# First attention of a two-block layer stack: outputs made transposed by pairs of heads, weights scaled before they are turned

## What is computed

```python
h = rms_norm(x, norm_gain);  proj = h @ w_in          # q, k, v, gates, z of both attentions
# NSA: 8 heads of 64 over 2 key groups, three branches
o_cmp = softmax(q kc^T, visible blocks) @ vc          # 32 compressed keys
o_sel = softmax(q ks^T, causal) @ vs                  # all 8 blocks are selected: plain causal
o_win = softmax(q kw^T, causal) @ vw                  # window 512: plain causal
nsa   = g0 * o_cmp + g1 * o_sel + g2 * o_win          # g: sigmoid gates per head and branch
# DSA: 8 heads, keys limited to the 128 best of an index score
dsa   = softmax(q_d k_d^T, causal and top 128) @ v_d
x     = x + concat(nsa * silu(z_n), dsa * silu(z_d)) @ w_out
```

## Time and profile before

| | us |
|---|---|
| median of 3 runs | 1799.81 (1799.48 to 1800.25) |
| the profiled execution | 1798.04 |
| its span in the trace | 1796.2 |
| first attention's loop on PE | 199.2 to 362.6 of the span |
| from there to the first matmul of the projection by w_out | 362.6 to 372.5 |
| projection by w_out | 372.5 to 424.5 |

### The profile page before, as it was taken

How to read it: one execution, slowest core, us unless ns; L and a number is a source line. 1 busy time by engine, 2 the same in 40 slices (tenths; PEclk the granted TensorE clock), 3 DMA queues, 4 the chain that set the end, 5 groups by cost and what they waited for, 6 DMA issues and landing times. The chain is left out here.

```text
span 1796.2 us, 23296 instructions
## 1 busy us (share of the span) xinstructions
PE 1734.0 (97%) x8345; PEld 1413.7 (79%) x8345; DVE 990.4 (55%) x1657; ACT 741.2 (41%) x1282; POOL 692.6 (39%) x301
## 2 busy tenths in 40 slices
PE   7999998988999999999999999999999999999997
PEld 7777787777888777788888888887776888888886
DVE  5999776475579687633333335789785631111112
ACT  6434555623375564322222223466464343222321
POOL 3424111236430234555545557440212544444442
PEclk9999999999999999999999999999999999999998
DMA  7234010053332224355555532332311222232211
GB/s 251 81 106 141 24 36 24 25 198 121 105 105 95 81 85 155 133 193 190 194 188 198 189 141 94 107 103 84 105 36 36 94 94 97 92 105 94 97 56 47
DMA packets 56633, 197.65 MB, mean 110 GB/s; under 512 B 6993, under 2 KB 8017, under 8 KB 56530
## 3 DMA queue, kind: packets, MB, share of 16 engines
q1 hardware_dynamic: 55666, 194.15, 31.8%
q10 hardware_dynamic: 864, 2.11, 0.3%
HBM read 194.14 MB, written 2.10 MB: 109 GB/s over the span
## 5 line engine op out<-in xcount | busy, mean ns | idle before, releaser
L513 POOL TENSOR_TENSOR WL<-RAW,WH 128x1024 fp32r<-128x1024 f32 x234 | 594.4, 2546 | 870.8 <-ACT WH L597 529.8
L1914 PE MATMUL bank<-HH,WH 128*128 128x512 f32 x1120 | 437.2, 390 | 9.5 <-POOLq L518 5.9
L1916 PE MATMUL bank<-HH,WL 128*128 128x512 f32 x1120 | 435.9, 389 | 0.0
L1915 PE MATMUL bank<-HL,WH 128*128 128x512 f32 x1120 | 435.8, 389 | 0.0
L597 ACT ACTIVATE WH<-RAW 128x1024 fp32r<-128x1024 f32 x259 | 270.6, 1052 | 244.2 <-PE bank L1916 220.0
L1914 PEld LDWEIGHTS bank<-HH,WH 128*128 128x128 f32 x1120 | 210.2, 188 | 55.1 <-issue 8.8
L1916 PEld LDWEIGHTS bank<-HH,WL 128*128 128x128 f32 x1120 | 210.2, 188 | 43.9
L1915 PEld LDWEIGHTS bank<-HL,WH 128*128 128x128 f32 x1120 | 210.3, 188 | 43.2
L1834 DVE TENSOR_TENSOR HF<-SILU,bank 128x512 f32<-128x512 f32 x43 | 29.6, 688 | 301.6 <-PE bank L1916 300.7
L1914 PE MATMUL bank<-HDH,WH 128*128 128x512 f32 x352 | 137.1, 389 | 0.0
L1916 PE MATMUL bank<-HDH,WL 128*128 128x512 f32 x352 | 136.9, 389 | 0.0
(11 more groups left out here) (371 smaller groups left out, 2934.5 us busy)
## 6 DMA issues: line engine op xcount, KB each, us to landing
RAW<-in_stream SPq DMA_DIRECT2D x363, 512.0 KB, 3.3
out_t<-YA SPq DMA_DIRECT2D x8, 256.0 KB, 2.2
X<-in_xt ACTq DMA_DIRECT2D x3, 512.0 KB, 10.9
RAW<-in_stream SPq DMA_DIRECT2D x2, 256.0 KB, 3.9
X<-in_xt ACTq DMA_DIRECT2D x2, 256.0 KB, 6.0
ACC<-in_pos SPq DMA_DIRECT2D x1, 256.0 KB
gains<-in_gains SPq DMA_DIRECT2D x1, 224.0 KB
CS<-in_cs SPq DMA_DIRECT2D x1, 128.0 KB
```

The source lines that it names most:

```text
L513: nc.gpsimd.tensor_tensor(lo(k)[:], raw(k)[:], hi(k)[:].bitcast(F32), ALU.subtract).then_inc(sem["passed"], mark("passed", *k))
L1914: nc.tensor.matmul(out, A[0], B[0], start=first, stop=False)
L1915: nc.tensor.matmul(out, A[0], B[1], start=False, stop=False)
L1916: return nc.tensor.matmul(out, A[1], B[0], start=False, stop=last)
```

## The change

- The units are ordered by head, then branch, then query tile, so that four units make one (head, branch) group. The weights of a unit are scaled by gate over sum while they still are in PR, before they are turned: by DVE for query tiles 0 and 1, by POOL for tiles 2 and 3. PR is a ring of eight, and the turn comes six turns behind the scores instead of three.
- The output of a whole group is four matmuls with V stationary (two columns of heads wide, the other head's columns zero in VZ) and the turned weights moving, 512, 384, 256 and 128 columns. Both heads of a pair and all branches accumulate in one bank, transposed, 128 by 512. The compressed branch is one matmul more per pair.
- Z is turned in the loop's turns 2 to 9, and DVE multiplies a pair's bank by it (`mix_pair_out`). MIX, its product on POOL and its turns are gone. High and low parts of a chunk are made as each pair ends, and the first matmuls of tiles 0 and 1 of the projection stand in the loop's last two turns.
- VZ has to be zero between the heads: POOL clears 128 x 3328 words before V is written.
- Compressed tiles start at turns 2, 6, 10, 14, the top-k rounds at turns 20 to 60. The 16 `ada` slots come in fours behind tiles 2 to 5 instead of in twos and threes behind tiles 0 to 5.

```diff
-        order += [ada.pop(0) for _ in range((2, 3, 3, 3, 3, 2, 0, 0)[n])]
+        order += [ada.pop(0) for _ in range((0, 0, 4, 4, 4, 4, 0, 0)[n])]
...
+UNITS1 = [(b, h % 4, h // 4, qt) for h in range(HEADS) for b in (0, 1) for qt in range(NT)]
+UNITS1 += [(2, h % 4, h // 4, qt) for h in range(HEADS) for qt in range(NT)]
+RING1, T_LAG1, O_LAG1 = 8, 6, 7
...
+def scaler(v):
+    return "p_norm" if v % NT < 2 else "p_pool"
+def mover(v):
+    return "read_dve" if v >= 20 and v % NT == 0 else "read_act"
+MIX_HI = {66: 0, 69: 1, 72: 2, 78: 3, 97: 4, 98: 5, 99: 6}
+MIX_LO_POOL = {66: 0, 69: 1, 72: 2, 77: 3}
+MIX_LO_DVE = {98: 4, 99: 5, 100: 6}
+O1_PASS = (76, 82, 90)
+O1_PARTS = {101: ((0, 0, 3),), 102: ((0, 3, 7), (1, 0, 7), (0, 7, 8), (1, 7, 8))}
...
# GpSimd, ahead of the projections and in the loop
+                    pool.wait_ge(sem["full"], value("full", "ti", 2))
+                    nc.gpsimd.memset(VZ[:], 0.0).then_inc(sem["pool_set"], mark("pool_set", "vz"))
...
+                if scaler(v) == "p_pool":
+                    pool.wait_ge(sem["p_inv"], value("p_inv", v))
+                    p_, over = PR[v % RING1][:, 0:n], COEF1[:, v % 16:v % 16 + 1]
+                    if br == 2:
+                        ins = nc.gpsimd.tensor_scalar(p_, p_, over, None, ALU.mult)
+                    else:
+                        col = 3 * (4 * g + j) + 1 + br
+                        ins = nc.gpsimd.tensor_scalar(p_, p_, over, gate[:, qt, col:col + 1], ALU.mult, ALU.mult)
...
# VectorE in the loop: evict_outputs goes, these come
+                    V.reciprocal(COEF1[:, v % 16:v % 16 + 1], RSUM1[:, v % 16:v % 16 + 1]).then_inc(
+                        sem["p_inv"], mark("p_inv", v))
+                    if scaler(v) == "p_norm":
...
+                            ins = V.tensor_scalar(p_, p_, over, gate[:, qt, col:col + 1], ALU.mult, ALU.mult)
...
+                V.tensor_tensor(gated(c), bank_of("oc", c)[:].rearrange("p (t q) -> p t q", t=NT), gated(c),
+                                ALU.mult).then_inc(
...
# TensorE in the loop
+                if 0 <= c < KD:
+                    turn(("tz", c), [Z[:, tt, c * P:(c + 1) * P] for tt in range(NT)])
...
+                    for kb in range(NT):
+                        last = nc.tensor.matmul(
+                            pair_bank[c][:, kb * P:S], VZ[:, kb, DH * m:DH * m + P], PT1[:, e % 2, kb, kb * P:S],
...
+                for n, k0, k1 in O1_PARTS.get(u, ()):
+                    o1_part(n, k0, k1)
...
-            for i in range(KD):
-                turn(("tm", i), [MIX[:, tt, i * P:(i + 1) * P] for tt in range(NT)])
```

More of the change, by code:

```diff
@@ L1508, in _ @@
+            pair_at = {pair_done(c) + 1: c for c in range(KD)}
             nU = len(UNITS1)
-            for u in range(nU + O_LAG):
+            for u in range(nU + O_LAG1):
                 if u < nU:
@@ L2124, in _ @@
             pe.wait_ge(sem["read_act"], value("read_act", "p1", 4, 3))
-            turn(("tc", 1), [G[4][:, tt, 384:512] for tt in range(NT)])
+            turn(("tc", 1), [VC[:, tt, :] for tt in range(NT)])
             project(3)
@@ L2182, in _ @@
                     full(last, "ct", qt)
-                qt = cmp_tile(u, CMP_PV)
-                if qt is not None:
-                    pe.wait_ge(sem["read_act"], value("read_act", "ct", qt))
-                    b = claim("cpv", qt)
-                    for g in range(2):
-                        last = nc.tensor.matmul(b[:, g * 256:(g + 1) * 256], PTC[:, qt % 2, g * P:(g + 1) * P],
-                                                VBLK[:, g, :], start=True, stop=True)
-                    full(last, "cpv", qt)
                 if u < nU:
@@ L2225, in _ @@
-            banks[0] = 8
-            pe.wait_ge(sem["gmix"], value("gmix", NT - 1))
-            for i in range(KD):
-                turn(("tm", i), [MIX[:, tt, i * P:(i + 1) * P] for tt in range(NT)])
-            def mix_pair(k):
-                if first_use("mix", k):
-                    pe.wait_ge(sem["read_dve"], value("read_dve", "tm", k))
-                return HH[:, k, :], HL[:, k, :]
+                e = group_at(u)
+                if e is not None:
+                    br, j, g, _ = UNITS1[NT * e]
+                    c = pair_of(e)
+                    first, end = pair_units(c)
+                    for name in ("read_act", "read_dve"):
+                        moved = [v for v in range(NT * e, NT * e + NT) if mover(v) == name]
+                        if moved:
+                            pe.wait_ge(sem[name], value(name, "t", 1, moved[-1]))
+                    if NT * e == first:
+                        pair_bank[c] = claim("oc", c, fixed=6 + c % 2)
+                    m = 2 * (2 * br + g) + 1 - j % 2
+                    for kb in range(NT):
+                        last = nc.tensor.matmul(
+                            pair_bank[c][:, kb * P:S], VZ[:, kb, DH * m:DH * m + P], PT1[:, e % 2, kb, kb * P:S],
+                            start=(kb == 0 and NT * e == first),
+                            stop=(kb == NT - 1 and c >= 4 and NT * e + NT - 1 == end))
+                    full(last, "o", 1, e)
+                    if c >= 4 and NT * e + NT - 1 == end:
+                        note[("full", "oc", c)] = count["full"]
@@ new lines, in _ @@
+                for c in range(4):
+                    if u == pair_done(c):
+                        if c == 0:
+                            pe.wait_ge(sem["read_act"], value("read_act", "ct", NT - 1))
+                        full(nc.tensor.matmul(pair_bank[c][:], VBLK[:, c // 2, P * (c % 2):P * (c % 2) + P],
+                                              PTC[:, c // 2, :], start=False, stop=True), "oc", c)
+                for n, k0, k1 in O1_PARTS.get(u, ()):
+                    o1_part(n, k0, k1)
@@ L2235, in _ @@
+            banks[0] = 8
             for n in range(KD):
[L2236 removed]
+                if n > 1:
+                    dense(("o1", n), [(("o1", n), P * k) for k in range(KD)], mix_pair)
                 mods(("o1", n))
```

252 lines of the change are left out of this document (144 added, 108 removed).

## The result

The changed kernel takes 1819.6 us (median of 4 runs, 1816.3 to 1820.1) against 1799.6 (1799.2 to 1800.3) beside it: ratio 1.0107, 95% interval 1.0095 to 1.0119. It is slower by 20 us; I had forecast 1795.0. Its profiled execution has a span of 1817.7 against 1796.2.

What follows compares the result with a forecast made beforehand. TensorE was taken to bound the kernel, except at the seam. -9.85 + 7.2 - 4.1 - 0.45 + 1.5 + 0.9 = -4.8 against 1798.04 gave 1793.2, plus 1.8 for the median 1795.0 us; range 1788.5 to 1802.

Steps and rivals of the forecast that it cites:

- The seam: Between loop and projection: Z's 32 turns and the waiting go, nothing becomes late there; -9.85 us.
- TensorE's work: In the loop: output groups 2.16 instead of 2.01, Z's eight turns 0.45 each; together +7.2 us, to +11.
- the 14 for the shared work: In the loop: about 14 us for compressed tiles, top-128 masks and modulation turns, which both kernels have.
- Waits in the loop: TensorE's small waits in the loop: 7.5 us instead of 11.6, so -4.1, bounds -8.6 and +8.
- The output's edge: Outputs need the previous unit's turned weights, 1.37 us of moving against 1.32 of cover; 0.1 a group, bounds 0 and 0.5.
- The filling: Loop's first ten turns: compressed tiles and Z's turns need banks that ScalarE must free; 2.5 us of waits.
- The scores' bank, three units back: In the loop: cover 1.95 us equals chain 1.9; as a rival, 0.4 a group gives 1802, chance 0.14.
- VectorE in the loop: Maxima, reciprocals, scalings, copy, product and top-128 take about 4.3 of TensorE's 5.9 us a group: hidden.
- GpSimd in the loop: Scalings of 512 words take 0.5 to 1.2 us; with `ada` sums it is busy 2.6 (to 3.0) of 5.9.
- The slower rival: VectorE and GpSimd exclude each other in the loop, 7.2 us a group against 5.9: +31 at most, 1826; chance 0.09.
- The clearing: Ahead of the loop: GpSimd's clearing of VZ may hold VectorE's chain, 0 to 3.1 us; taken as +1.5.
- The projection: After the loop: waits for `ada` sums at tiles 4, 5 and 6, 6.5 us in all; +0.9, bounds -2 and +5.

Runs made afterwards that it cites:

- c2: c1 with the gate's eight turns at turns 18, 21, ... 39 of the loop instead of 2 to 9: 1794.5 us.
- f2: c2 with projection sums spread 2, 4, 4, 4, 2, first modulation turns at 73, every scaling on GpSimd with two factors: 1786.4 us.
- c1: Changed kernel with the clearing split, outputs one turn later, and GpSimd's low parts behind the last `ada` sum: 1795.2 us.
- a3: Changed kernel with each group's outputs one turn later, a lag of 8 turns instead of 7: 1805.3 us.
- b1: Kernel before the change with only GpSimd's clearing of 3328 words added: 1806.1 us, ratio 1.0033.
- a1: Changed kernel with the clearing split, two tiles at the kernel's start, only zero blocks of the others at the old place: 1814.7 us.

## Why the prediction was wrong, point by point

- *The seam*: right, -9.85, and nothing became late there.
- *TensorE's work*: right. Output groups without a wait issue for 2.16, Z's turns for 0.44 (in c2). f2's loop of 160.1 with 3.6 us of waits leaves at most 156.5 of work where I had 159.0, so I forgot nothing; the 14 for the shared work was rather too much (137.6 and 14 also make 151.6, not 151.8), and the waits of both kernels are larger than my terms have them by as much.
- *Waits in the loop*: the step that failed. In the prediction's own terms they were 27.6 us (11.6 before, and 23.2 of added loop less 7.2 of work) instead of 7.5, by two terms of the sum. The output's edge was seen and its numbers were nearly right (1.37 of moving against 1.32 of cover), but I priced it at 0.1 a group. It measured some 0.45, at the upper bound of 0.5. Where chain and cover are equal, side work on the engine in between (`ada` scalings, high parts) is paid nearly in full, 0.4 to 1.2 us each time it falls there, and the equality itself costs 0.2 to 0.3. I had put that side work into one lump of 2.0. The filling was some 13 instead of 2.5: 1.6 for the crowding (c2 against c1), about 4 for the clock, the rest waits, most of them for ScalarE's moves; a3, at a clock of 1.00, still loses some 7 there with the longer lag. That they passed from one bank to the next I only infer. My walk stopped at turn 7.
- *The scores' bank, three units back*: the rival that it paces the loop had no part. Waits for it (exponentials) are 1.4 us.
- *VectorE in the loop, GpSimd in the loop*: hidden, as forecast. The range for GpSimd's 512 words, 0.5 to 1.2, missed the one-factor form's 1.56; it had turns to spare.
- *The slower rival*, that the engines exclude each other in the loop: a small part at most, 6 holds of 48 and 1.2 us of waits behind one of them. The result lies near its 1826 for other reasons.
- *The clearing*: the second step that failed. I had +1.5 for it; b1, with nothing else added, has +8.4 at the first score (the changed kernel +7.8, as its start was right: about -0.6 instead of -0.45). I took the clearing's own length as the upper bound, 3.1. The direct hold is 1.34; the damage came from the meetings after it. A bound for something that delays a chain with many meetings must allow for whole further holds.
- *The projection*: +2.1 instead of +0.9; waits 6.2 where I had 6.5, the rest the clock at 0.97.
- *Range*: 1802 as upper end left out exactly the upper bounds that the text itself named, 12 instead of 2.4 for the edge. With that bound the waits' terms come to 17.1, +5.5 against the kernel before; the text gives +8, and it was +16.

## What to carry to other kernels

Where the work that covers a chain is only as long as the chain, price each item of side work on the engine in between at its full length, and give one more turn of lag if the buffers allow it: here a constant changed by one was worth 14 us, some 4 of them by the clock of the first turns. An instruction added to GpSimd is to be looked at against every VectorE operation on SBUF until the next point where TensorE waits, not only against the one beside it; clear early, and only what isn't written later. When a large change disappoints, test its small new constants and placements first: with a few of them moved, the idea itself was good.

## What the hardware showed

- A GpSimd clearing, which only writes, held a VectorE `TENSOR_SCALAR` of 128 words (1.57 us for 0.23 at 59.13) and not the three `SCALAR_TENSOR_TENSOR` at 58.15 (0.95; 0.94 in the kernel before). A subtraction on GpSimd held both kinds (63.94, 69.87), and a sum held a `TENSOR_SCALAR` (262.78). The Trainium skill (SBUF — State Buffer, Who interferes with whom) says so: an operation with two SBUF inputs contends only with GpSimd instructions that read, one in a two-port mode, which `tensor_scalar` can be, with any. This trace agrees: 1.57 us for the one, 0.95 for the other.
- GpSimd's `TENSOR_SCALAR` on 512 fp32 words takes 1561 ns with one factor, 774 with two from SBUF and 691 with one from SBUF and the constant 1.0 (384 words: 1242, 660, 584).
- The clearing of 3328 words took 2.88 us, the one of 896 words in blocks of 64 0.84 to 0.85.
- The first matmul after a wait costs about 0.1 us more: output groups 2.26 with one, 2.16 without.
- TensorE's granted clock in the loop's first 51 to 54 us was 0.87, 0.93, 0.97 or 1.00, also between kernels of the same loop (0.87 in the changed one, 1.00 in a1), and moved the loop by up to 4 us. Spells at half clock followed waits such as the 7.35 us at 92.57; what decides about the others stays open. a3's ten runs lie 10.6 us apart (1797.4 to 1808.0). The slower ones had the lower clock over the whole run, 0.986 to 0.989 in the six from 1804.5 up and 0.992 in the two at 1797.5; the profile, taken near the median, doesn't show where the difference falls.
